# Expert weights of experts 3 and 4 loaded in shifted half chunks, and the final norm's weight spread by products instead of a DMA

## What is computed

```python
u = rmsnorm(h, norm_mix_w); p = u @ w_in
h += (sigmoid(g_pool) * pool_branch + sigmoid(g_dn) * deltanet_branch) @ w_out
# experts: 4 groups of 8, top-1 group, then top-2 experts inside it, width 512
u = rmsnorm(h, norm_ffn_w)
logits = u @ w_grp + b_grp, u @ w_rtr + b_rtr
for e in range(32):
    y += comb[:, e] * ((silu(u @ w_gate[e]) * (u @ w_up[e])) @ w_down[e])
h += y
out = rmsnorm(h, norm_final_w)[:, 16:]
```

## Time and profile before

| | us |
|---|---|
| median of 3 runs | 775.12 |
| lowest, highest | 774.88, 775.59 |
| the profiled execution | 776.95 |
| its span, first to last instruction | 775.2 |
| TensorE busy in the span | 748.8 (97%) |
| VectorE, ScalarE, GpSimd busy | 320.9, 311.9, 125.4 |
| granted TensorE clock, mean share of full speed | 0.996 |

### The profile page before, as it was taken

One profiled execution on the slowest core, in us unless ns is written; L12 is line 12 of the kernel. 1 busy time (PEld: TensorE's weight loads), 2 busy tenths in 40 slices (PEclk: granted clock), 3 DMA queues, 4 the chain that ended last, 5 costly groups with the idle time before them and its releaser, 6 DMA issues.

```text
span 775.2 us, 16094 instructions
## 1 busy us (share of the span) xinstructions
PE 748.8 (97%) x6512; PEld 536.1 (69%) x6512; DVE 320.9 (41%) x793; ACT 311.9 (40%) x632; POOL 125.4 (16%) x209
## 2 busy tenths in 40 slices
PE   8999999999999999899999999999999999998895
PEld 7989989998999988655555555565555555454452
DVE  4894687678675855822211311220221112111112
ACT  6975678586584744712212121222112121121123
POOL 7473242225433540000000000000000000000000
PEclk9999999999999999999999999999999999999999
DMA  8536556554754458999999999999999999999993
GB/s 204 147 87 165 152 135 160 138 151 110 181 147 125 140 193 309 414 400 424 420 427 428 428 427 428 425 429 426 428 427 427 428 427 426 429 426 426 424 416 137
DMA packets 83552, 241.06 MB, mean 311 GB/s; under 512 B 7185, under 2 KB 65666, under 8 KB 71826
## 3 DMA queue, kind: packets, MB, share of 16 engines
q1 hardware_dynamic: 83170, 239.19, 81.2%
q10 hardware_dynamic: 304, 0.79, 0.4%
HBM read 238.92 MB, written 1.05 MB: 310 GB/s over the span
## 4 chain that ended last, share of the span: by engine, by line
PE 80%; DMA 11%; issue 4%; DVE 4%; ACT 1%; POOL 0%; SPq 0%; DVEq 0%; POOLq 0%; ACTq 0%
PE banks L2158 23%; PE banks L1811 21%; PE banks L2216 12%; DMA ring<-in_expert_w_up_dram 10%; PE banks L2089 3%; PE banks L2171 3%; PE banks L2007 2%; PE banks L1931 1%; PE banks L2192 1%; PE banks L1944 1%; PE banks L1992 1%; PE banks L1935 1%; DMA x<-in_x_dram 1%; PE banks L1969 1%; PE banks L1948 1%
## 5 line engine op out<-in xcount | busy, mean ns | idle before, releaser
L2158 PE MATMUL banks<-ring,bench 128*64 128x256 f32 x2048 | 240.0, 388 | 8.4 <-DMA ring<-in_expert_w_up_dram 6.2
L2158 PEld LDWEIGHTS banks<-ring,bench 128*64 128x64 f32 x2048 | 146.6, 134 | 108.8 <-issue 21.0
L1811 PE MATMUL banks<-rounded 128*128 128x256 f32 (+2 forms) x1320 | 194.1, 294 | 0.0
L1811 PEld LDWEIGHTS banks<-rounded 128*128 128x128 f32 x1320 | 168.5, 189 | 3.1
L1714 DVE TENSOR_TENSOR bench<-banks,bench 128x256 f32<-128x256 f32 x32 | 13.6, 425 | 259.5 <-PE banks L2158 172.2
L2216 PE MATMUL banks<-ring,bench 128*64 128x512 f32 x512 | 116.9, 598 | 0.6 <-ACT bench L1096 0.5
L1107 ACT ACTIVATE ysb<-banks 64x512 f32<-64x512 f32 x63 | 37.2, 591 | 147.2 <-PE banks L2216 146.5
L2216 PEld LDWEIGHTS banks<-ring,bench 128*64 128x64 f32 x512 | 34.1, 136 | 63.2 <-issue 59.4
L875 ACT ACTIVATE rounded<-room 128x1024 fp32r<-128x1024 f32 x64 | 67.4, 1054 | 23.2 <-PE banks L1811 15.1
L1096 ACT ACTIVATE bench<-banks 128x256 f32<-128x256 f32 x32 | 12.3, 384 | 146.9 <-PE banks L2192 146.9
L1333 DVE TENSOR_TENSOR rounded<-room,rounded 128x1024 fp32r<-128x1024 f32 x49 | 61.6, 1259 | 16.5 <-ACT rounded L875 15.5
(11 more groups left out here) (312 smaller groups left out, 867.0 us busy)
## 6 DMA issues: line engine op xcount, KB each, us to landing
ring<-in_expert_w_down_dram SPq DMA_DIRECT2D x28, 2048.0 KB, 26.7
ring<-in_expert_w_gate_dram SPq DMA_DIRECT2D x27, 2048.0 KB, 25.6
ring<-in_expert_w_up_dram SPq DMA_DIRECT2D x27, 2048.0 KB, 26.8
room<-in_w_in_dram SPq DMA_DIRECT2D x56, 512.0 KB, 4.3
ring<-in_expert_w_up_dram SPq DMA_DIRECT2D x16, 512.0 KB, 7.1
ring<-in_expert_w_down_dram SPq DMA_DIRECT2D x16, 512.0 KB, 7.1
ring<-in_expert_w_gate_dram SPq DMA_DIRECT2D x12, 512.0 KB, 5.8
room<-in_w_out_dram SPq DMA_DIRECT2D x8, 512.0 KB, 4.5
```

The source lines that it names most:

```text
L1811: ins = T.matmul(o, a, b[:, k, lo_at:L], start=(k == 0 and n == 0), stop=(k == KT - 1 and n == 2))
L2158: ins = T.matmul(pb[5 + c][half * 64:half * 64 + SLOTS, 0:256], xgT[:, q % ROOMS, kt, j * SLOTS:(j + 1) * SLOTS], w[:, kt, half], start=(k ...
```

## The change

- The chunks 9 to 14 (experts 3 and 4) are loaded in halves, and each half goes half a place earlier than the chunk would: the first half of chunk 9 into `spare` (all of it, 128 x 2048), its second half into the first half of place 0, the first half of chunk 10 into the second half of place 0, and so on. `half_at` gives the place, for the load and for the products.
- The first half of chunk 9 is issued when the logits of both token halves are done. The other halves wait for the finished chunk (`used_up`) or for the new semaphore `half`, which TensorE raises in the middle of each of the chunks 0 to 14. The quarters and the semaphore `quarter` are gone.
- From chunk 15 on chunks are whole again. A chunk n with n - 8 in 9 to 14, thus 17 to 22, waits for `half` too.
- `wfin` moves from `spare` to the second half of `xgT`'s room 0. Its DMA and the wait before it are gone. Instead the weight is loaded at the start as `gain_out`, 128 x 8 floats like `gain`, and at experts 28 and 29 TensorE multiplies each column of it, broadcast to 128 columns, by half of the identity (8 products of 64 columns each expert, into bank 4, `spread_gain`, behind `turn_mid`), and VectorE copies 128 x 512 to `wfin`.
- The landing of `gain` and `gain_out` now counts in `bias_land` with the two small loads before them; all who waited for one of these wait for all four. This adds a wait to ScalarE's step "ea" and VectorE's step "xa" near the start.
- `landed` counts loads by the new function `loads_until`. For expert 0 it waits for none.

The core of the diff:

```diff
-QUARTERED = [(RINGS, 0), (RINGS, 1), (RINGS, 2), (RINGS + 1, 2)]
+RING = 3 * RINGS
+SHIFTED = range(RING, RING + 6)
+HALF_COUNTED = range(RING + 6)
+GAIN_PARTS = 2
...
+def loads_of(n, again):
+
+    if (n // 3, n % 3) in PIECES or n < 3 and not again:
+        return 0
+    if n in SHIFTED and not again:
+        return 2
+    return QUARTERS if n in (3, 4) and not again else 1
...
-        wfin = spare[:, D:2 * D]
         gain = sb("gain", [P, KT])
+        gain_out = sb("gain_out", [P, KT])
...
+        wfin = xgT[:, 0, KT // 2:KT, :].rearrange("p k s -> p (k s)")
...
+        def half_at(n, half, again):
+
+            if n in SHIFTED and not again:
+                at = 2 * (n - RING) + half - 1
+                if at < 0:
+                    return spare[:]
+            else:
+                at = 2 * (n % RING) + half
+            return ring[:, RING_AT[at // 2], at % 2 * CHUNK // 2:(at % 2 + 1) * CHUNK // 2]
...
-            sp.dma_start(gain[:], norm_ffn_w[0].rearrange("(p k) -> p k", k=KT)).then_inc(S("gain_land"), 16)
+            sp.dma_start(gain[:], norm_ffn_w[0].rearrange("(p k) -> p k", k=KT)).then_inc(S("bias_land"), 16)
+            sp.dma_start(gain_out[:], norm_final_w.rearrange("(p k) -> p k", k=KT)).then_inc(S("bias_land"), 16)
...
-                    taken(sp, ("G", HEADS - 1))
-                    sp.dma_start(wfin, norm_final_w[None, :].to_broadcast([P, D])).then_inc(S("rout_land"), 16)
...
+                for n in range(3 * EXPERTS):
+                    e, c = n // 3, n % 3
+                    if n in SHIFTED and not again:
+                        if n == RING:
+                            sp.wait_ge(S("logits"), TT)
+                        else:
+                            used_up(n - RING - 1)
+                        if n >= RING + 3:
+                            sp.wait_ge(S(f"w_land{n - RING}"), 16 * loads_until(n - RING, False))
+                        load_half(sp, n, 0)
+                        sp.wait_ge(S("half"), n - RING + 1)
+                        load_half(sp, n, 1)
+                        continue
+                    if n >= RING:
+                        used_up(n - RING)
+                        if n - RING + 1 in SHIFTED and not again:
+                            sp.wait_ge(S("half"), n - RING + 2)
+                    elif again:
+                        sp.wait_ge(S(used[c]), base)
+                    if again or (e and (e, c) not in EARLY):
+                        load_chunk(sp, e, c)
...
                 if kind == "ea":
-                    act.wait_ge(S("bias_land"), 2 * 16)
+                    act.wait_ge(S("bias_land"), 4 * 16)
...
+                    elif j < GAIN_PARTS:
+                        dve.wait_ge(S("gathered"), parts + QUADS * PARTS + j + 1)
+                        V.tensor_copy(wfin[:, j * 512:(j + 1) * 512], pb[4][:]).then_inc(S("xgT"), 1)
...
+                def spread_gain(n):
+
+                    pe.wait_ge(S("xgT"), parts + QUADS * PARTS + n - 2)
+                    for k in range(KT):
+                        ins = T.matmul(pb[4].rearrange("p (j k) -> p k j", k=KT)[:, k, :], gain_out[:, k:k + 1].to_broadcast([P, P]),
+                                       ident[:, n * 64:(n + 1) * 64], start=True, stop=True, skip_group_check=True)
+                    ins.then_inc(S("gathered"), 1)
...
-                        if first and (kt + 1) % (KT // QUARTERS) == 0 and kt < KT - 1:
-                            ins.then_inc(S("quarter"), 1)
+                        if kt == KT // 2 - 1 and 3 * e + c in HALF_COUNTED and not again:
+                            ins.then_inc(S("half"), 1)
...
                     if q + 1 < QUADS:
                         gather(q + 1, j, 1)
+                    elif j < GAIN_PARTS:
+                        spread_gain(j)
                     if g == 0 and i:
                         spread(i - 1)
                     down(e)
```

More of the change, by code:

```diff
@@ L79 @@
 ROOMS = 2
-ROUT = 5 * 16
+ROUT = 4 * 16
 XRES = 3 * 16
@@ L417, with loads_until, loads_in_all @@
         LO_AT[_s[1]] = (_name, _i + 1)
-def uses(n, k, slots):
-    return (n - k + slots - 1) // slots
+def loads_of(n, again):
[4 more added lines that the diff above has]
+    return QUARTERS if n in (3, 4) and not again else 1
+def loads_until(n, again):
+    return sum(loads_of(m, again) for m in range(n % RING, n + 1, RING))
+def loads_in_all(slot, again):
+    return sum(loads_of(m, again) for m in range(slot, 3 * EXPERTS, RING))
 def build_block(nc, x, meta_tokens, norm_mix_w, w_in, conv_w, pool_w, pool_scale, a_log, dt_bias, dn_norm_w,
@@ L812, in one_pass @@
                 again = not isinstance(ps, int)
[L813 to L831, removed]
@@ L1655, in one_pass @@
                 again = not isinstance(ps, int)
-                experts, pairs, parts = EXPERTS * ps, PAIRS * ps, QUADS * PARTS * ps
+                experts, pairs, parts = EXPERTS * ps, PAIRS * ps, (QUADS * PARTS + GAIN_PARTS) * ps
                 def slots_of(q):
@@ L2124, in landed @@
                 def landed(e, c):
-                    short = sum(k == c and n % RINGS == e % RINGS for n, k in PIECES)
-                    if e == 0 and not again:
-                        pe.wait_ge(S(f"first_land{c}"), 4 * 16)
-                        return
-                    loads = ps * (uses(EXPERTS, e % RINGS, RINGS) - short) - (e % RINGS == 0)
-                    quarters = QUARTERS - 1 if e % RINGS == 0 or e % RINGS == 1 and (c < 2 or again or e > RINGS) else 0
-                    pe.wait_ge(S(f"w_land{3 * (e % RINGS) + c}"), 16 * (loads + quarters + (e // RINGS + 1)))
+                    n = 3 * e + c
+                    loads = loads_until(n, again)
+                    if again:
+                        first, other = (loads_in_all(n % RING, over) for over in (False, True))
+                        loads = ps * other + (first - other + loads)
+                    pe.wait_ge(S(f"w_land{n % RING}"), 16 * loads)
                 def gate_up(e, c, name):
@@ L2148, in gate_up @@
                             pe.wait_ge(S("give"), pairs + i)
-                    w = ring[:, RING_AT[3 * (e % RINGS) + c], :].rearrange("p (k q h j) -> p k h q j", k=KT, h=2, j=2)
+                    ws = [half_at(3 * e + c, n, again).rearrange("p (k q h j) -> p k h q j", k=KT // 2, h=2, j=2) for n in range(2)]
                     for kt in range(KT):
@@ L2210, in down @@
                         landed(e, 2)
-                    w = ring[:, RING_AT[3 * (e % RINGS) + 2], :].rearrange("p (j d) -> p j d", j=4)
+                    ws = [half_at(3 * e + 2, n, again).rearrange("p (j d) -> p j d", j=2) for n in range(2)]
                     for j in range(4):
```

21 lines of the change are left out of this document (14 added, 7 removed).

## The result

The changed kernel takes 777.58 us (median; 776.86 to 779.34) beside 775.12 for the kernel before on the same chip: ratio 1.0031, interval 1.0021 to 1.0041, so 2.5 us slower. It is 1.3 us above the forecast of 776.3, on the side of "slower" where I had put most of the chance on "same". It lies inside the range by 0.02 us only (773.9 to 777.6), and the same kernel measured again took 777.77, outside it: that the first figure fell inside is luck.

The account below looks back on a forecast made before the run. The prediction took TensorE to bind until 615 us, then the stream of expert weights. Stream +0.1, products +1.05 and start 0 gave +1.15 on 775.12, so 776.3 us, range 773.9 to 777.6.

Parts of the forecast that it names:

- The bound: Expert stage: TensorE alone until 615 us, then the stream of expert weight DMAs at about 427 GB/s.
- The front gain: Chunks 9 to 16: earlier halves and the removed final weight DMA put the stream 2.2 us ahead at chunk 16.
- given back at chunk 17: Chunk 17's new wait moves its issue from 367.33 to 369.14; it lands 7.45 us later, so all front gain is gone.
- The step that failed: Stream after chunk 17: landing at 376.6 instead of 376.5, so +0.1 us, bounds 0.45 early to 0.65 late.
- Later waits don't bind: Waits behind chunk 17 cost nothing: chunk 22, the next narrowest, could land at 400.0, its turn being 401.1.
- The products: Experts 28 and 29: 3.4 us of products, 2.0 of it held by the slack of two waits; +1.05 carried.
- X: TensorE time of the 16 product records per expert at experts 28 and 29: 1.72 us, from above 2.06.
- The start: ScalarE's first exponential now waits for `gain_out`, landing about 16.2 behind its table load: cost 0, up to 0.8 if later.
- A: Rival: products cost their upper 1.75 and the late issue its 0.65; TensorE holds experts 28 to 31; 777.5; chance 0.19.
- B: Rival: the front gain lasts, the extra wait at chunk 17 being covered; 774.0, or 772.9 with hidden products; chance 0.15.
- C: Rival: the change does nothing, gain given back and products hidden in TensorE's waits; 775.2; chance 0.12.
- D: Rival: the wait at the start moves everything by 0.7 us; 777.0; chance 0.06.

Follow-up runs that it names:

- n_late9: n_rot, with the first half of chunk 9 also waiting for the middle of gate(0); 774.39 us, ratio 0.9989 to the kernel before.
- n_rot: Changed kernel with chunks 9 to 18 in halves, later ones one place lower, no wait longer than before; final weight by end DMA, no products; 773.33 us.
- a_late9: Changed kernel, with the first half of chunk 9 also waiting for the middle of gate(0); 777.92 us, ratio 1.0037 to the kernel before.
- a_endload: Changed kernel without the products; the final weight comes by one DMA behind the last piece of weights; 776.15 us, ratio 1.0011 to the kernel before.
- b_waits: Kernel before, with only the changed kernel's longer waits of chunks 17 to 22 added; 776.18 us, ratio 1.0015.
- b_only17: Kernel before, with only the longer wait of chunk 17 added; 776.41 us, ratio 1.0012.
- a_no17: Changed kernel, in which chunk 17 doesn't wait for `half`; 777.75 us, ratio 1.0025 to the kernel before.
- n_prod: n_rot with the changed kernel's products for the final weight instead of the end DMA; 775.44 us, ratio 0.9997 to the kernel before.
- b_late: Kernel before with only the change's late part: products at experts 28 and 29, final weight's early DMA gone; 776.86 us, ratio 1.0021.
- a_shift9: Changed kernel with nine chunks (9 to 17) in shifted halves instead of six, longer waits from chunk 18; 776.59 us, ratio 1.0021 to the kernel before.

## Why the prediction came out as it did

**The bound** was read rightly: TensorE to 615 us, then the stream. Time of the stream counts at the end nearly in full: n_late9 had fetched 0.65 MB, 1.5 us, less than n_rot by 356 us, up(28) came 1.3 later, and the median is 1.06 higher. TensorE's 3.4 us of products cost 0.9 to 1.6.

**The front gain** was put at 2.2 us. n_rot, which keeps it, is 2.05 below the kernel before and has up(28) 2.2 earlier. Of these the early half of chunk 9 is 1.06; the rest the runs don't divide further. The size was right. That the changed kernel would still have all of it at chunk 16 was not: there 0.8 was left (44.9 for 45.7), since chunk 15 had already come too late for the stream. It made no difference to the time, as the late issue of chunk 17 bound whatever had been won ahead of it.

**That it is given back at chunk 17** was right in place and time: issued 43.29 after gate(0), landing 7.6 after issue. a_late9 shows that nothing of the early half is left at experts 28 to 31. The Trainium skill (DMA: Bandwidth & Descriptors, "Anatomy of one DMA") gave an estimate of 6.8 for a lone chunk. Its formula is fitted to DMAs that GpSimd issues, which the prediction doesn't say; these are SyncE's, and took 7.4 to 7.6 where the queue had run dry (a_endload, b_waits, changed).

**The step that failed is the size of what is left: +0.1 (bounds -0.45 and +0.65), measured +0.7 to +1.05.** I compared landing with landing, 376.6 with 376.5. But a landing counts when the last of 16 DMA engines is through. In the trace's records of before, chunk 17 is through on the first engine 48.8 after gate(0) and on the last 50.6; in b_waits at 50.1 and 50.8, in b_only17 at 50.2 and 51.4. The last engine lost 0.2 and 0.7, the first 1.3 and 1.5: before, the other engines had been ahead of the last, and they lost that lead. up(28), some 340 us on, came 0.6 and 0.7 later. The read rate, the mean over all 16, gives 0.85 us of stream in b_only17 and 14 GB/s x 30 us = 0.42 MB or 1.0 us in b_waits. Both are about the loss in time; for b_waits, as for the changed kernel (50.9 for 50.7), the landing sum was not. That the lost lead is what costs is read from these records; no run changes it alone.

**"Later waits don't bind"** held only behind a late chunk 17. I had tested chunk 22 against a stream that had already been made late at chunk 17, and with that it holds: b_only17 is no better than b_waits. But taking the wait of 17 away (a_no17) leaves a stream that is 2 us earlier, for which chunks 18 and 19 are too late in their turn. A wait that binds hides the next one. The prediction could have seen it: it called chunk 22 the next narrowest, with 1.1 us to spare, but chunk 19, issued 52.3 after gate(0) (378.2 by the clock of before), could land at 385.6 by the same sum, and its turn is 376.6 + 2 x 4.9 = 386.4. It had 0.8.

**The products.** X was put at 1.72 an expert: 1.73 in the chain after, 0.108 us a record. (The Trainium skill, TensorE: Matmul & The Clock Gate, "Back-to-back issue gap", has about 81 ns for sustained pairs with 128 moving columns; this kernel's records disagree with it as the logits' did.) The walk through the tail gave +1.05, and from up(28) to down(31) the traces have 0.9 to 1.2. That term was right. The medians have more: 1.4 to 1.6, 1.5 and 2.1. For n_prod the two groups of executions explain it in part. For the other two pairs the rest, some 0.4 to 0.65 us, lies ahead of up(28), in the stream. In b_late it is the 0.65 that come with the final weight's DMA gone. In the changed kernel up(28) starts at 388.59 and 388.55 in two profiles against 388.11 in a_endload, which has the same loads up to there; no product has run yet, and the cause stays open.

**The start** cost nothing, as predicted. ScalarE around its step "ea" in the changed kernel, in order of time (its table load, and the operation that now waits for four small loads; the earlier trace rows):

```profile
15.25 1.28 ACT L958 ACT_TABLE_LOAD   x1
16.55 0.21 ACT L958 ACTIVATE bc<-bc 96x8 f32<-96x8 f32 x1
```

**The sum** is then 0.7 + 1.6 + 0 = 2.3 for the 2.46 measured, where I had 0.1 + 1.05 + 0. By the traces it is 1.1 in the stream up to up(28) and 1.1 behind: most of what the forecast missed, 1.0 of 1.3 us, lies in the stream. **The rivals:** A's time (777.5) is the measured one, by half of its reason: the late issue did cost its upper 0.65, but the products were not longer than 1.73. B (the gain lasts) is excluded by a_endload, which has no products and is still slower than the kernel before, C by a_endload and b_late, D by the rows above. The bounds of the stream term took in only the fixed part of one DMA; what a pause does to the 15 engines that are ahead of the slowest stood in no term.

## What to carry to other kernels

What loading earlier at the front wins is given back, in part (a_shift9) or in full (changed), at each later issue that is not as early against the stream as it was; list the issues of a whole round of the ring with their new waits, and look for the next one behind the first that binds, before counting a gain. Where a shift of half a place makes waits longer, turn the places once more (n_rot) so that each chunk's old neighbours are free when it comes: that kept the 2 us. And a product that fills a buffer is no free replacement of a DMA behind the last load: near the end, where each expert has only some 0.3 to 0.8 us of slack, 3.4 us of products over two experts cost a quarter to a half of their length, and 3.6 us more nearly all of theirs.

## What the runs showed of the hardware

- A queue that runs dry can cost more than the landing of the next DMA tells: the 16 engines reach the end of a chunk at different times (1.9 us apart at chunk 17 of the kernel before, 3.0 at chunk 30, 5.5 at chunk 80), and a pause takes away the lead of those ahead. In b_waits an issue 1.8 us later (43.31 for 41.46 after gate(0)) moved the last engine's end of chunk 17 by 0.2 us and the first's by 1.3; the kernel is 0.8 slower.
- After a pause the first packets are slow. In the changed kernel the first 15 of chunk 17, 16 KB each, start 44.3 to 44.9 after gate(0), 1.0 to 1.6 behind the issue, and take 1.0 to 1.8 us; between 100 and 200 us after gate(0), where the queue is never empty, the median is 0.61.
- An fp32 product with 64 moving columns and 128 x 128 stationary costs what one with the logits' 36 columns does: 0.108 us a record (1.73 for 16) and 0.111 for each further one (3.68 - 1.90 for 16), against 0.1075 in the earlier trace rows. Between these two the number of moving columns doesn't change the price.
- In these profiles, one execution each, the mixer ends at one of two times: gate(0) starts at 324.0 to 324.6 or at 325.8 to 325.9. It is not the kernel that decides (b_waits 324.04, b_only17 325.79), and n_prod's executions fall into two groups about as far apart; so it seems to vary from execution to execution, which moves single profiles and medians of 10. What decides was not tried.
